# A chunked delta-rule recurrence on Trainium2: when the transposes, the norm's variance sums and the last inverse are issued, and where ScalarE copies the transposes

## The chip, the cores and the metric

The kernel runs on one core of one Trainium2 chip. The metric is the device time of one execution, in microseconds (us); the time before is the median of three runs.

## The reference

The program computes two blocks on a sequence of 512 tokens of width 1024, in float32. The first block has an RWKV-7 mixer (32 heads of size 64) and a short convolution; the second has a gated convolution, stick-breaking attention and a gated FFN. The change touches only the mixer's recurrence and the norm behind it:

```python
def wkv7_scan(r, decay, k, v, kk, kka):
    def step(S, inp):
        r_t, w_t, k_t, v_t, kk_t, kka_t = inp
        sa = jnp.einsum('bhvk,bhk->bhv', S, kk_t)
        S = (S * w_t[:, :, None, :] - sa[..., None] * kka_t[:, :, None, :]
             + v_t[..., None] * k_t[:, :, None, :])
        return S, jnp.einsum('bhvk,bhk->bhv', S, r_t)
...
def head_group_norm(y, w, b):
    mu = jnp.mean(y, axis=-1, keepdims=True)
    var = jnp.mean(jnp.square(y - mu), axis=-1, keepdims=True)
    yn = (y - mu) * lax.rsqrt(var + GN_EPS)
...
    y = wkv7_scan(rh, heads(decay), kh, vh, kk, kk * ah)
    y = head_group_norm(y, lnx_w, lnx_b)
    y = (y + bonus) * jax.nn.silu(g)
    return y @ w_out, v_first
```

## The kernel before

Most of the program is dense products of float32 numbers split into a high and a low part (lines 1948 to 1950). Between about 429 and 829 us runs the recurrence. It is chunked: 8 chunks of 64 tokens; within a chunk the step-by-step update becomes products of matrices and the inverse of a unit triangular matrix, and only a 64x64 state per head goes from chunk to chunk.

The 32 heads are cut into 8 turns of four heads (`PAIRS` = 8; two 128-row tiles `a` of two heads `h`). The loop has turns t = 0 to 8 and in each of them 24 steps s = 0 to 23. Three stages overlap as a pipeline:

- **Preparation of turn t.** It is done in four groups n (tile a, half g of the chunks, table `GROUPS`). For each group TensorE forms the products of queries and keys, `products` (line 576, 8 matmuls of 128 columns, 16 records), and transposes keys and values, `transposes` (lines 588 and 591, 8 matmuls). They work in PSUM banks 0 to 3 in alternation: products of group n use banks 2 and 3 where n is even and 0 and 1 where it is odd, transposes the other pair. So products of n wait until ScalarE has copied the transposes of n-1 (`turned_copied`), and transposes of n wait until VectorE has masked the products of n-1 (`products_masked`). VectorE masks with `first_steps` at step 2n and `second_steps` at step 2n+1 (lines 937 to 952). ScalarE copies the transposes in `turned_out` (bt, sv: 3 or 4 copies by the helper on line 832) and rounds in `rounded` (nixd, line 832). Steps 9 to 21 invert: `first_inverse`, five levels of `newton_v` (line 613, even steps) and `newton_x` (line 599, odd steps), whose results VectorE (`w`, line 1005, and one of four `inv`, line 787) and ScalarE (three of four `inv`) copy, then `residual` at step 20 and `last_inverse` at 21, whose results go into `tt`.
- **Chain of turn t-1.** `chain(t-1, s // 3, s % 3)`: each chunk takes three steps. Phase 0 (lines 523, 509, 529) forms the right side, phase 1 (line 542) multiplies it by the inverse `tt`, phase 2 (lines 550, 556) updates the state. After each phase `recurrence_evac` copies the result out of PSUM, half of the rows by VectorE (lines 758, 771) and half by ScalarE (line 759): `rhs`, then `sv` as u, then `sv` as the next state (two small copies on ScalarE). The next phase on TensorE waits for both halves.
- **Norm of turn t-2.** `norm_sum` (lines 690 and 693, one 128x512 float32 sum each in bank 4) centers and takes the variance of two tiles; ScalarE copies `sq`, squares into `acc` (line 904) and makes the inverse deviation (lines 908, 909); GpSimd ends the tile in `finish` (lines 1059 to 1062).

Each engine executes its own list in the order written, and a wait holds back all that stands behind it. TensorE's list in a step is: chain, then preparation, then norm sum. ScalarE's is: its part of the chain, `y_out` (the copy `tmp` of the y bank 7, line 832) at steps 0 and 12, its part of the preparation, its part of the norm:

```python
                    if when(t - 1, PAIRS):
                        recurrence_evac(act, 1, t - 1, s // 3, s % 3)
...
                    if when(t, PAIRS):
                        if s in (1, 3, 5, 7):
                            turned_out(t, s // 2)
                            rounded(t, s // 2)
```

SP issues the loads of later turns; each waits for the stage that frees its tile (`turned`, `y_summed`, `y_finished`).

Of the kernel before, what the change touches and what calls it, by code (L numbers as in the profile page):

```python
# [142 lines left out]
def program(nc, i, out):  # L143

    with ExitStack() as ctx:
# [340 lines left out]
        S_FIRST, S_LEVELS, S_RESIDUAL, S_LAST = 9, 10, 20, 21  # L486
        GROUPS = [(0, 0), (1, 0), (0, 1), (1, 1)]
        TURNED = [3, 6, 10, 14]

# [8 lines left out]
        def recurrence_tensor(pe, out_part):  # L498
# [62 lines left out]
            def products(t, n):  # L561

                (a, g), b = GROUPS[n], t % 2
                if n == 0:
                    pe.wait_ge(R["front_loaded"][b], LOAD_Q * (t // 2 + 1))
                    pe.wait_ge(R["keys_loaded"], LOAD_BC * (t + 1))
                    if t:
                        for h in range(2):
                            pe.wait_ge(R["inverse_made"][h], 2 * t)
                else:  # L570
                    if n == 2:
                        pe.wait_ge(R["back_loaded"][b], LOAD_Q * (t // 2 + 1))
                    pe.wait_ge(R["turned_copied"], TURNED[3] * t + TURNED[n - 1])
                for c in range(4):
                    for h in range(2):
                        last = mm(bank[product_bank(n, h)][:, c * P:(c + 1) * P], st_bc[rows[h], a, 4 * g + c, :, :],  # L576
                                  st_q[b][rows[h], a, h:h + 2, 4 * g + c, :], start=True, stop=True)
                last.then_inc(R["products_summed"], 1)

            def transposes(t, n):  # L580

                a, g = GROUPS[n]
                if n == 0:
                    pe.wait_ge(R["values_loaded"], LOAD_V * (t + 1))
                else:
# [71 lines left out]
            def last_inverse(t):  # L657

                for n, (a, g) in enumerate(GROUPS):
# [43 lines left out]
            for t in range(PAIRS + 1):  # L703
                for s in range(3 * NCH):
                    if t == 0 and s == 1:
                        pe.wait_ge(s_free[0], U_OUT1 // 2)
                        pe.wait_ge(s_free[1], U_OUT1 // 2)
# [81 lines left out]
        def recurrence_scalar(act, o, out_weights):  # L789
# [71 lines left out]

            for t in range(PAIRS + 2):
                b, q = t % 2, t - 2
                for s in range(3 * NCH):
                    if when(t - 1, PAIRS):
# [3 lines left out]
                    if s == 12 and when(t - 1, PAIRS):  # L869
                        y_out(t - 1, 0)  # L870
                    if when(t, PAIRS):
                        if s in (1, 3, 5, 7):
                            turned_out(t, s // 2)
# [19 lines left out]
                        elif s == S_LAST:  # L893
                            for n in range(2):
                                act.wait_ge(R["t_summed"], 4 * t + n + 1)
                                copy(tt[b][:, n, 0:4, :], heads(n)).then_inc(R["inverse_made"][0], 1)
                    if when(q, PAIRS):
                        if s in (2, 6):
                            a = s // 6
                            act.wait_ge(R["centered"], 2 * q + a + 1)  # L900
                            if q:
                                act.wait_ge(R["y_finished"], 2 * q - 1 + a)
                            o(copy(yc[a], bank[4][:]))
                            A(ysq[:], yc[a], ACT.Square).then_inc(R["y_squared"], 1)
                        if s in (4, 8):
                            a = s // 8
                            act.wait_ge(R["var_summed"], 2 * q + a + 1)
                            o(A(yr[a][:], bank[4][:], ACT.Ln, bias=eps[:, 1:2]))
                            A(yr[a][:], yr[a][:], ACT.Exp, scale=-0.5).then_inc(R["y_rstd_made"], 1)
                    then(t, s)  # L910

        def recurrence_vector(dve, o, out_weights):
# [66 lines left out]
            for t in range(PAIRS + 1):  # L979
                b = t % 2  # L980
                for s in range(3 * NCH):
# [34 lines left out]
                    elif s == S_LAST:  # L1016
                        for n in (2, 3):
                            dve.wait_ge(R["t_summed"], 4 * t + n + 1)
# [31 lines left out]
        def recurrence_gpsimd(gp, o):  # L1050
# [22 lines left out]
            for t in range(PAIRS + 2):  # L1073
# [5 lines left out]
                if when(t - 2, PAIRS):  # L1079
                    finish(t - 2, 0)  # L1080
# [3 lines left out]
                if when(t - 2, PAIRS):  # L1084
                    finish(t - 2, 1)
# [1662 lines left out]
```

## Time and profile before

| | |
|---|---|
| median of 3 runs | 2080.65 us (2079.68 to 2084.85) |
| profiled execution | 2086.95 us, its span 2085.2 us |
| TensorE busy (matmuls) | 2000.9 us, 96% |
| VectorE, ScalarE, GpSimd busy | 1395.0, 1032.0, 190.1 us |
| recurrence, turns 0 to 8 | about 429.6 to 829 us of the span |

The profile describes one execution. A busy share says how full an engine was, not what it held up; which engine sets the pace in a stretch is read from the waits in the timeline and from the chain of waits. In a timeline row the first number is the start, the second the time to the end of the last of the merged instructions; in brackets stands the idle time of the engine ahead of it and what ended it. A matmul shows twice: PEld is its weight load, PE the matmul itself. Matmul records of float32 count in passes (x16 for 8 matmuls of the program).

### The profile page before, as it was taken

What the parts mean: (1) busy time and instruction counts of PE and PEld (TensorE: products, weight loads), DVE (VectorE), ACT (ScalarE), POOL (GpSimd) and SP (SyncE); (2) the same over time, 40 slices, a digit from 0 to 9 for tenths busy, and PEclk for the clock granted to TensorE, in tenths of its full rate; (3) what the DMA queues carried; (4) which work ended last, traced back from release to release, by engine and by line L of the source; (5) the groups of instructions that cost most, each with busy time, mean ns of one, the idle gap of its engine ahead of it and who ended that gap; (6) DMA issues with size and microseconds to landing.
All of it is one profiled execution on the core that took longest, in us unless ns stands there. A gap on an engine that the chain in (4) does not pass through costs nothing.

```text
span 2085.2 us, 40330 instructions
## 1 busy us (share of the span) xinstructions
PE 2000.9 (96%) x15310; PEld 1609.8 (77%) x15310; DVE 1395.0 (67%) x2240; ACT 1032.0 (49%) x1829; POOL 190.1 (9%) x214
## 2 busy tenths in 40 slices
PE   5999999988889899999999999999999999999998
PEld 4877777777777776888888888888667778888886
DVE  7788888886566564555554556799777776455455
ACT  6666666666677675333322323442675434233243
POOL 4230000021343222100000000000000000000000
PEclk9999999999999999999999999999999999999999
DMA  4445555562334312233333333333113323333332
GB/s 120 119 142 162 178 185 174 176 155 75 95 84 99 81 56 82 87 96 94 97 101 92 100 91 100 101 91 100 40 43 107 95 61 91 97 95 95 97 93 78
DMA packets 371367, 215.02 MB, mean 103 GB/s; under 512 B 52369, under 2 KB 349737, under 8 KB 371241
## 3 DMA queue, kind: packets, MB, share of 16 engines
q1 hardware_dynamic: 371032, 213.18, 35.1%
q8 instruction: 91, 1.49, 0.3%
q14 instruction: 36, 0.29, 0.0%
q10 hardware_dynamic: 208, 0.06, 0.0%
HBM read 181.68 MB, written 31.52 MB: 102 GB/s over the span
## 4 chain that ended last, share of the span: by engine, by line
PE 88%; ACT 5%; DVE 4%; issue 2%; DMA 1%; SPq 1%; ACTq 0%; DVEq 0%
PE bank L1948 24%; PE bank L1950 23%; PE bank L1949 23%; PE bank L599 2%; PE bank L576 2%; PE bank L613 1%; PE bank L550 1%; PE bank L509 1%; ACT inv L832 1%; PE bank L523 1%; PE bank L588 1%; PE bank L1138 1%; PE bank L542 1%; PE bank L690 1%; PE bank L591 1%
## 5 line engine op out<-in xcount | busy, mean ns | idle before, releaser
L1948 PE MATMUL bank<-xl,w_hi 128*128 128x512 f32 x1568 | 615.6, 393 | 3.5 <-DVE xl L2670 2.5
L1949 PE MATMUL bank<-xl,w_lo 128*128 128x512 f32 x1568 | 611.2, 390 | 0.0
L1950 PE MATMUL bank<-xl,w_hi 128*128 128x512 f32 x1568 | 610.9, 390 | 0.0
L1595 ACT ACTIVATE w_hi<-w_raw 128x1024 fp32r<-128x1024 f32 x278 | 293.1, 1054 | 481.4 <-PE bank L1950 476.9
L2239 DVE TENSOR_TENSOR w_lo<-w_raw,w_hi 128x1024 fp32r<-128x1024 f32 x278 | 342.2, 1231 | 48.7 <-ACT w_hi L1595 40.1
L1948 PEld LDWEIGHTS bank<-xl,w_hi 128*128 128x128 f32 x1568 | 294.5, 188 | 76.6 <-issue 9.9
L1950 PEld LDWEIGHTS bank<-xl,w_hi 128*128 128x128 f32 x1568 | 294.8, 188 | 61.8
L1949 PEld LDWEIGHTS bank<-xl,w_lo 128*128 128x128 f32 x1568 | 294.7, 188 | 60.6 <-issue 0.5
L1948 PE MATMUL bank<-xh,w_hi 128*128 128x512 f32 x448 | 182.8, 408 | 12.2 <-DVE xh L2244 11.9
L1950 PE MATMUL bank<-xh,w_hi 128*128 128x512 f32 x448 | 175.2, 391 | 0.0
L1949 PE MATMUL bank<-xh,w_lo 128*128 128x512 f32 x448 | 175.0, 391 | 0.0
L1948 PEld LDWEIGHTS bank<-xh,w_hi 128*128 128x128 f32 x448 | 84.5, 189 | 33.9 <-issue 9.1
L1949 PEld LDWEIGHTS bank<-xh,w_lo 128*128 128x128 f32 x448 | 84.6, 189 | 18.1 <-issue 0.7
L1950 PEld LDWEIGHTS bank<-xh,w_hi 128*128 128x128 f32 x448 | 84.4, 188 | 17.9
L2514 DVE SCALAR_TENSOR_TENSOR dconv<-glu,par,dconv 128x512 f32<-128x512 f32 x120 | 83.1, 748 | 0.5
L832 ACT ACTIVATE inv<-bank 128x512 f16<-128x512 f32 (+1 forms) x152 | 73.3, 553 | 18.7 <-PE bank L599 16.8
L2244 DVE TENSOR_TENSOR xl<-tmp,xl 128x512 f32 (+1 forms) x62 | 42.1, 689 | 33.0 <-ACT xl L1923 17.9
L1005 DVE CAST_PREDICATED w<-bmask,bank 128x256 f16<-128x256 int32 x160 | 56.5, 417 | 6.7 <-PE bank L613 4.8
L787 DVE CAST inv<-bank 128x512 f16<-128x512 f32 x40 | 27.7, 692 | 44.9 <-PE bank L599 44.9
L1948 PE MATMUL bank<-y_part,w_hi 128*128 128x512 f32 x128 | 52.8, 413 | 0.0
L599 PE MATMUL bank<-inv,w 64*64 64x64 f16 x1280 | 46.7, 197 | 5.7 <-issue 5.7
L599 PE MATMUL bank<-w,inv 64*64 64x64 f16 x1280 | 47.3, 198 | 4.1 <-issue 3.9
(385 smaller groups left out, 3084.5 us busy)
## 6 DMA issues: line engine op xcount, KB each, us to landing
w_raw<-in_a_w_in SPq DMA_DIRECT2D x64, 512.0 KB, 4.2
w_raw<-in_b_w_in SPq DMA_DIRECT2D x64, 512.0 KB, 4.1
w_raw<-in_w_ffn_up SPq DMA_DIRECT2D x42, 512.0 KB, 3.9
w_raw<-in_w_in SPq DMA_DIRECT2D x36, 512.0 KB, 3.8
w_raw<-in_a_w_out SPq DMA_DIRECT2D x16, 512.0 KB, 3.8
w_raw<-in_b_w_out SPq DMA_DIRECT2D x16, 512.0 KB, 3.7
w_raw<-in_w_ffn_down SPq DMA_DIRECT2D x16, 512.0 KB, 3.7
d_g<-sq SPq DMA_DIRECT2D x16, 256.0 KB, 2.2
```

The costliest lines, as they stand in the source:

```text
L576: last = mm(bank[product_bank(n, h)][:, c * P:(c + 1) * P], st_bc[rows[h], a, 4 * g + c, :, :], st_q[b][rows[h], a, h:h + 2, 4 * g + c, :] ...
L599: last = mm(bank[n][hs, col0 + c * C:col0 + (c + 1) * C], lhsT[hs, 4 * g + c, :], rhs_[hs, 4 * g + c, :] if rhs_ is not eyes16 else eyes16 ...
L787: return copy(inv2[a][:, :, 4 * g:4 * g + 4, :], bank[n][:].rearrange("p (x c k) -> p x c k", x=2, c=4))
L832: return A(dst, src, ACT.Copy)
L1005: V.copy_predicated(w16[a][:, 4 * g:4 * g + 4, :], bmask[:, level, :].bitcast(I32).unsqueeze(1).to_broadcast([P, 4, C]), heads(n)).then_in ...
L1595: A(w_hi[0:rows, slot, 0:nkb, 0:ncol], w_raw[0:rows, slot, 0:nkb, 0:ncol], ACT.Copy).then_inc(s_hi, units)
L1948: mm(outp, wh, xlo, start=start, stop=False)
L1949: mm(outp, wl, xhi, start=False, stop=False)
L1950: return mm(outp, wh, xhi, start=False, stop=stop)
L2239: V.tensor_tensor(w_lo[part], w_raw[part], w_hi[part].bitcast(F32), ALU.subtract).then_inc(s_lo, units)
L2244: V.tensor_tensor(lo, tmp[:, buf, :], hi.bitcast(F32), ALU.subtract).then_inc(s_xlo, 1)
L2514: V.scalar_tensor_tensor(out=y, in0=glu[:, j, tap:tap + T], scalar=w, in1=y, op0=ALU.mult, op1=ALU.add).then_inc(s_tap, 1)
```

## The change

Nothing is computed otherwise; five things are issued in another order.

1. TensorE: `transposes` of group n follow `products` of the same group directly, at step 2n; they stood at step 2n+1.
2. ScalarE: `turned_out` of groups 1 to 3 stands at step 2n ahead of that step's `recurrence_evac`; `turned_out` of group 0 stands at step 0 behind it. `rounded` stays at step 2n+1. The `y_out` of step 12 moves to step 11.
3. Norm, in turns t < 8: the sums that center stay at steps 1 and (from 5 as before) 5, the sums of squares go from steps 3 and 7 to 11 and 15; on ScalarE center at 2 and 6, square at 4 and 14, inverse deviation at 12 and 16 (they were at 2, 6, 4 and 8, with the square right behind the centering). In turn 8 the steps stay as they were. GpSimd's `finish` of tile 0 moves behind its two `low_part`.
4. `last_inverse` is split: groups 2 and 3 at step 21, 0 and 1 at step 22; ScalarE's two copies `tt` go with the latter.
5. Waits follow: the products of a turn wait only for VectorE's half of the `tt` copies, the transposes for ScalarE's.

```diff
         S_FIRST, S_LEVELS, S_RESIDUAL, S_LAST = 9, 10, 20, 21
+        LAST_GROUPS = {S_LAST: (2, 3), S_LAST + 1: (0, 1)}
+        SUMS_LATE = {1: (0, False), 5: (1, False), 11: (0, True), 15: (1, True)}
+        SUMS_EARLY = {1: (0, False), 3: (0, True), 5: (1, False), 7: (1, True)}
+        NORM_LATE = {2: ("center", 0), 4: ("square", 0), 6: ("center", 1), 12: ("rstd", 0), 14: ("square", 1),
+                     16: ("rstd", 1)}
+        NORM_EARLY = {2: ("center_square", 0), 4: ("rstd", 0), 6: ("center_square", 1), 8: ("rstd", 1)}
...
 (products, n == 0)
-                        for h in range(2):
-                            pe.wait_ge(R["inverse_made"][h], 2 * t)
+                        pe.wait_ge(R["inverse_made"][1], 2 * t)
 (transposes, n == 0)
+                    if t:
+                        pe.wait_ge(R["inverse_made"][0], 2 * t)
...
 (norm_sum)
+                late = q + 2 < PAIRS
                 if not squares:
                     pe.wait_ge(R["y_bank_read"], 2 * q + 2)
-                    if q or a:
+                    if late and a:
+                        pe.wait_ge(R["y_squared"], 2 * q + 1)
+                    elif q or a:
                         pe.wait_ge(R["y_rstd_made"], 2 * q + a)
...
                 else:
+                    if late and a:
+                        pe.wait_ge(R["y_rstd_made"], 2 * q + 1)
+                    elif late:
+                        pe.wait_ge(R["r0_copied"], 4 * (q + 3))
                     pe.wait_ge(R["y_squared"], 2 * q + a + 1)
...
 (TensorE's step)
-                        if s < 8:
-                            (transposes if s % 2 else products)(t, s // 2)
-                            if t == 0 and s % 2:
-                                fill(4)
+                        if s < 8 and s % 2 == 0:
+                            products(t, s // 2)
+                            transposes(t, s // 2)
+                        elif s < 8 and t == 0:
+                            fill(4)
...
-                        elif s == S_LAST:
-                            last_inverse(t)
-                    if when(t - 2, PAIRS) and s in (1, 3, 5, 7):
-                        norm_sum(t - 2, s // 4, s % 4 == 3)
+                        elif s in LAST_GROUPS:
+                            last_inverse(t, LAST_GROUPS[s])
+                    if when(t - 2, PAIRS) and s in sums_of(t):
+                        norm_sum(t - 2, *sums_of(t)[s])
...
 (ScalarE's step)
+                    if when(t, PAIRS) and s in (2, 4, 6):
+                        turned_out(t, s // 2)
                     if when(t - 1, PAIRS):
                         recurrence_evac(act, 1, t - 1, s // 3, s % 3)
...
-                    if s == 12 and when(t - 1, PAIRS):
+                    if s == 11 and when(t - 1, PAIRS):
                         y_out(t - 1, 0)
                     if when(t, PAIRS):
-                        if s in (1, 3, 5, 7):
-                            turned_out(t, s // 2)
+                        if s == 0:
+                            turned_out(t, 0)
+                        elif s in (1, 3, 5, 7):
                             rounded(t, s // 2)
```

How the lists of the engines move is shown at two places of turn 2, which stands for turns 2 to 7. First ScalarE, steps 1 to 3, before: L759 is its part of the chain (waits `u_summed`, `s_summed`, `rhs_summed`), `bt` and `sv_132` the copies of the transposes (`turned`), `nixd` the rounding, `sq` and `acc` the norm.

```order
L759 ACTIVATE sv_133<-bank 64x2x64 [waits u_summed]
L832 ACTIVATE bt_144<-bank 128x512 [waits turned]
L832 ACTIVATE sv_132<-bank 64x4x64 x2
L832 ACTIVATE nixd_125<-nix_134 64x4x64 [waits nix_made]
L832 ACTIVATE nixd_125<-nix_134 64x4x64
L759 ACTIVATE sv_133<-bank,st_pc_140 64x64 [waits s_summed]
L759 ACTIVATE sv_133<-bank,st_pc_140 64x64
L832 ACTIVATE sq<-bank 128x512 [waits centered]
L904 ACTIVATE acc<-sq 128x512 [waits scalar_order]
L759 ACTIVATE rhs<-bank 64x128 [waits rhs_summed]
L832 ACTIVATE bt_144<-bank 128x512 [waits turned]
L832 ACTIVATE sv_132<-bank 64x4x64 x2
```

The same engine in the change (its helper lines are 781 for 759, 854 for 832), from step 0's copy of the transposes to step 3's right side:

```order
L854 ACTIVATE bt_144<-bank 128x512 [waits turned]
L854 ACTIVATE sv_132<-bank 64x4x64 x2
L781 ACTIVATE sv_133<-bank 64x2x64 [waits u_summed]
L854 ACTIVATE nixd_125<-nix_134 64x4x64 [waits nix_made]
L854 ACTIVATE nixd_125<-nix_134 64x4x64
L854 ACTIVATE bt_144<-bank 128x512 [waits turned]
L854 ACTIVATE sv_132<-bank 64x4x64 x2
L781 ACTIVATE sv_133<-bank,st_pc_140 64x64 [waits s_summed]
L781 ACTIVATE sv_133<-bank,st_pc_140 64x64
L854 ACTIVATE sq<-bank 128x512 [waits centered]
L781 ACTIVATE rhs<-bank 64x128 [waits rhs_summed,scalar_order]
```

The copies of group 1 (the second `bt`) stood behind the state copies and the rhs copy; they stand ahead of both.

Second TensorE, the same place in the change: steps 2 and 3 (L562 and L568 are phase 2 of the chain, L587 products, L604 and L607 transposes, L535 phase 0 of the next chunk).

```order
L562 MATMUL bank<-sv_132,bt_144 64x64 [waits u_copied1,u_copied0]
L562 MATMUL bank<-sv_132,bt_144 64x64 x3
L568 MATMUL bank<-ra_143,sv_132 64x64 x4
L587 MATMUL bank<-st_q_129,st_bc 128x128 [waits turned_copied]
L587 MATMUL bank<-st_q_129,st_bc 128x128 x7
L604 MATMUL bank<-ident,st_bc 128x128 [waits products_masked]
L604 MATMUL bank<-ident,st_bc 128x128 x3
L607 MATMUL bank<-ident,st_v 128x128 x4
L535 MATMUL bank<-sv_132,st_q_128 64x64 [waits s_copied1,s_copied0]
```

Before, L523 (now L535) with its wait for both state copies stood between L576 and L588, and a sum of squares (L693) behind L591.

## Rows read from the trace of the kernel before

**Rows 1.** The page: busy time, share and instructions of TensorE and ScalarE.
```profile
PE 2000.9 (96%) x15310; PEld 1609.8 (77%) x15310; DVE 1395.0 (67%) x2240; ACT 1032.0 (49%) x1829; POOL 190.1 (9%) x214
```
**Rows 2.** Stretches: length, busy of PE, PEld, DVE, ACT, POOL, clock; turns 1 and 3.
```profile
463.12:508.85 45.73, 38.03 (x985) 32.30 (x982) 30.20 (x84) 28.38 (x79) 6.95 (x8) 1.00 0.29 73
...
557.59:603.62 46.03, 41.37 (x994) 33.51 (x992) 28.55 (x81) 32.97 (x86) 15.31 (x15) 1.00 0.33 84
```
**Rows 3.** Stretches of turn 3: steps 0 to 8, 9 to 19; turn 1's steps 0 to 8.
```profile
557.59:576.92 19.33, 18.06 (x242) 13.30 (x239) 13.67 (x38) 15.45 (x42) 6.93 (x7) 1.00 0.15 39
576.92:597.80 20.88, 18.20 (x593) 15.58 (x593) 12.04 (x35) 14.91 (x38) 7.22 (x7) 1.00 0.58 149
...
463.12:482.97 19.85, 15.25 (x234) 12.39 (x229) 15.33 (x41) 12.13 (x37) 3.69 (x5) 1.00 0.05 10
```
**Rows 4.** Timeline of turn 3, steps 2 to 4, TensorE and ScalarE.
```profile
561.87 0.45 PE L550 MATMUL bank<-sv,bt 128*64 128x64 f32 x8
...
562.49 1.16 PE L576 MATMUL bank<-st_q,st_bc 64*128 64x128 f32 x16
...
563.61 0.54 PE L523 MATMUL bank<-sv,st_q 128*64 128x64 f32 x8
...
564.67 0.65 PE L588 MATMUL bank<-ident,st_bc 128*128 128x128 f32 x4
...
565.60 1.02 PE L693 MATMUL bank<-acc,head_mean 128*128 128x512 f32 x2
565.80 0.60 ACT L832 ACTIVATE bt<-bank 128x512 f32<-128x512 f32 x1 [0.55 <-PE bank L591]
...
566.55 0.45 PE L542 MATMUL bank<-rhs,tt 64*64 64x64 f32 x8
567.09 0.85 ACT L832 ACTIVATE nixd<-nix 64x256 f16<-64x256 f32 x2
```
**Rows 5.** Timeline of turn 3: GpSimd in step 5, the waits ahead of step 9.
```profile
569.57 1.28 POOL L1059 TENSOR_TENSOR y<-sq,yr_a 128x512 f32<-128x512 f32 x1 [11.97 <-ACT yr_a L909]
...
576.49 0.50 ACT L759 ACTIVATE sv<-bank,st_pc 64x64 f32<-64x64 f32 x2
...
576.92 0.54 PE L523 MATMUL bank<-sv,st_q 128*64 128x64 f32 x8 [1.07 <-ACT sv L759]
577.20 0.69 ACT L908 ACTIVATE yr_b<-bank,eps 128x512 f32<-128x512 f32 x1
```
**Rows 6.** Timeline of turn 3's inversion: steps 12 and 13, then 15 to 17.
```profile
584.17 0.45 PE L509 MATMUL bank<-st_q,sv 64*64 64x64 f32 x8 [0.51 <-ACT tmp L832]
...
589.87 0.42 PE L542 MATMUL bank<-rhs,tt 64*64 64x64 f32 x8
...
590.91 0.27 ACT L759 ACTIVATE sv<-bank 64x128 f32<-64x128 f32 x1
590.95 0.41 PE L613 MATMUL bank<-inv,nixd 128*128 128x64 f16 x8 [0.20 <-ACT inv L832]
591.82 0.51 ACT L759 ACTIVATE sv<-bank,st_pc 64x64 f32<-64x64 f32 x2 [0.63 <-PE bank L550]
```
**Rows 7.** Timeline of turn 3, steps 21 to 23, last inverse and what follows.
```profile
602.15 0.42 PE L542 MATMUL bank<-rhs,tt 64*64 64x64 f32 x8
...
603.11 0.45 PE L550 MATMUL bank<-sv,bt 128*64 128x64 f32 x8 [0.53 <-DVE sv L758]
```
**Rows 8.** Stretches by TensorE's clock: busy, then clock, DMA share, GB/s.
```profile
683.30:686.70 3.40, 1.60 (x76) 1.00 0.47 136
686.70:690.10 3.40, 3.17 (x45) 0.50 0.02 5
```
**Rows 9.** Timeline of TensorE: a product of the inversion at either clock.
```profile
583.02 0.64 PE L613 MATMUL bank<-inv,nixd 128*128 128x64 f16 x16
...
686.93 0.32 PE L599 MATMUL bank<-inv,w 64*64 64x64 f16 x4 [2.03 <-issue]
...
688.86 1.04 PE L613 MATMUL bank<-inv,nixd 128*128 128x64 f16 x16
```

More of the change, by code:

```diff
@@ L486, in program, with sums_of, norm_of @@
         S_FIRST, S_LEVELS, S_RESIDUAL, S_LAST = 9, 10, 20, 21
+        LAST_GROUPS = {S_LAST: (2, 3), S_LAST + 1: (0, 1)}
         GROUPS = [(0, 0), (1, 0), (0, 1), (1, 1)]
         TURNED = [3, 6, 10, 14]
+        SUMS_LATE = {1: (0, False), 5: (1, False), 11: (0, True), 15: (1, True)}
[3 more added lines that the diff above has]
+        NORM_EARLY = {2: ("center_square", 0), 4: ("rstd", 0), 6: ("center_square", 1), 8: ("rstd", 1)}
+        def sums_of(t):
+            return SUMS_LATE if t < PAIRS else SUMS_EARLY
+        def norm_of(t):
+            return NORM_LATE if t < PAIRS else NORM_EARLY
         def when(turn, last):
@@ L584, in transposes @@
                     pe.wait_ge(R["values_loaded"], LOAD_V * (t + 1))
+                    if t == 0:
+                        pe.wait_ge(s_free[0], U_OUT1 // 2)
+                        pe.wait_ge(s_free[1], U_OUT1 // 2)
+                    if t:
+                        pe.wait_ge(R["inverse_made"][0], 2 * t)
                 else:
@@ L655, in residual, with last_inverse @@
                     both_heads(n, nixd[a], inv2[a][:, 0], start=False).then_inc(R["e_summed"], 1)
-            def last_inverse(t):
-                for n, (a, g) in enumerate(GROUPS):
+            def last_inverse(t, groups):
+                for n in groups:
+                    a, g = GROUPS[n]
                     pe.wait_ge(R["e_copied"][n // 2], 2 * t + n % 2 + 1)
@@ L704, in recurrence_tensor @@
                 for s in range(3 * NCH):
-                    if t == 0 and s == 1:
-                        pe.wait_ge(s_free[0], U_OUT1 // 2)
-                        pe.wait_ge(s_free[1], U_OUT1 // 2)
                     if when(t - 1, PAIRS):
@@ L860, in y_out, with norm_part @@
                      bank[7][:].rearrange("p (a t) -> p a t", a=2)).then_inc(R["y_bank_read"], 1)
+            def norm_part(q, part, a):
+                if part.startswith("center"):
+                    act.wait_ge(R["centered"], 2 * q + a + 1)
+                    if q:
+                        act.wait_ge(R["y_finished"], 2 * q - 1 + a)
+                    o(copy(yc[a], bank[4][:]))
+                if part.endswith("square"):
+                    act.wait_ge(R["var_summed"], 2 * q + a)
+                    A(ysq[:], yc[a], ACT.Square).then_inc(R["y_squared"], 1)
+                if part == "rstd":
+                    act.wait_ge(R["var_summed"], 2 * q + a + 1)
+                    o(A(yr[a][:], bank[4][:], ACT.Ln, bias=eps[:, 1:2]))
+                    A(yr[a][:], yr[a][:], ACT.Exp, scale=-0.5).then_inc(R["y_rstd_made"], 1)
             for t in range(PAIRS + 2):
@@ L892, in recurrence_scalar @@
                                 copy(w16[n][:, 0:4, :], heads(n)).then_inc(R["e_copied"][0], 1)
-                        elif s == S_LAST:
+                        elif s == S_LAST + 1:
                             for n in range(2):
-                                act.wait_ge(R["t_summed"], 4 * t + n + 1)
+                                act.wait_ge(R["t_summed"], 4 * t + n + 3)
                                 copy(tt[b][:, n, 0:4, :], heads(n)).then_inc(R["inverse_made"][0], 1)
[L897 to L909, printed above, removed]
+                    if when(q, PAIRS) and s in norm_of(t):
+                        norm_part(q, *norm_of(t)[s])
                     then(t, s)
@@ L1017, in recurrence_vector @@
                         for n in (2, 3):
-                            dve.wait_ge(R["t_summed"], 4 * t + n + 1)
+                            dve.wait_ge(R["t_summed"], 4 * t + n - 1)
                             V.tensor_copy(tt[b][:, n - 2, 4:8, :], heads(n)).then_inc(R["inverse_made"][1], 1)
@@ L1078, in recurrence_gpsimd @@
                         G.tensor_copy(w16[a][:], eyes[:]).then_inc(R["units_reset"], 1)
-                if when(t - 2, PAIRS):
-                    finish(t - 2, 0)
                 if when(t, PAIRS):
@@ L1084, in recurrence_gpsimd @@
                 if when(t - 2, PAIRS):
+                    finish(t - 2, 0)
                     finish(t - 2, 1)
```

## The prediction

> **What bounds the kernel now.** I read the page first, for the size of things: TensorE is busy 96% of the span [rows 1]. That share is an average over dense products, which the change does not touch, and the recurrence. So next come the stretches of the recurrence, one turn each: turn 1, still without the norm, takes 45.73 us, a middle turn (turn 3) 46.03, with TensorE busy 41.37 and ScalarE 32.97 [rows 2]. Cut by steps [rows 3], its steps 0 to 8 take 19.33 us with TensorE busy 18.06 and ScalarE 15.45; steps 9 to 19, the inversion, take 20.88 with TensorE busy 18.20. So in steps 0 to 8 TensorE is nearly full, and every new wait there is added time; in the inversion a little room is left. The timeline then shows what the order does. Between phase 2 of the chain (561.87), the products (562.49), the next phase 0 (563.61), the transposes (564.67), the sum (565.60) and phase 1 (566.55) TensorE does not stop [rows 4]: while ScalarE and VectorE copy one thing, TensorE has another. The one long wait is at the end, 1.07 us ahead of 576.92, for ScalarE's state copies [rows 5].
>
> **The prices.** Issue time on TensorE, start to start [rows 4]: phase 2 of the chain 0.62, products 1.12, phase 0 1.06, transposes 0.93, a sum 0.95; phase 1 about 0.33 (its row's 0.45 less the latency; 0.28 more for line 509 every fourth chunk; phase 0 of a turn's first chunk only 0.70, as it lacks line 509). The transposes' result reaches ScalarE 1.13 after they start (564.67 to 565.80), so 0.20 after their last issue. `turned_out` then takes 1.29 (565.80 to 567.09), `rounded` 0.85 [rows 4]; the copy of a right side or of u 0.27 [rows 6], the pair of state copies 0.50 [rows 5]. From ScalarE's end to TensorE's start I take 0.1 to 0.2, the 0.20 of [rows 6].
>
> **Part 1, transposes and ScalarE's order, steps 0 to 8.** TensorE issues at an even step chain, products, transposes, and at the next odd step needs ScalarE's half of that chain part. ScalarE may copy it only behind `turned_out` of the same step, which waits for the transposes, although the chain's result has been there for two us. I lay the prices out from the start of the turn:
> - Step 0: phase 0 to 0.70, products to 1.8, transposes to 2.7. ScalarE copied the right side at 0.45 (here the chain is first), so phase 1 follows to 3.35 and the centering sum to 4.3. ScalarE: transposes' result 2.94, `turned_out` to 4.23, u copy to 4.5. TensorE starts phase 2 at 4.7: it waits 0.4.
> - Step 2: phase 2 to 5.3, products to 6.4, transposes to 7.36, result 7.56. `turned_out` to 8.85, the state copies to 9.4. TensorE waits from 7.36 to 9.45: 2.1 us.
> - Steps 3 and 4: phase 0 to 10.45, phase 1 to 10.85, products and transposes to 12.9, result 13.1; `turned_out` (four copies now, 1.33) to 14.4, u copy 14.7. TensorE goes on at 14.9: 2.0.
> - Steps 5 and 6: phase 2 and the second centering sum to 16.5, phase 0, products and transposes to 19.5, result 19.7, `turned_out` 21.05, right side 21.4. TensorE goes on at 21.5: 2.0.
> - Steps 7 and 8: phase 1 to 21.9, u copy by 22.3, phase 2 from 22.5 to 23.1; `rounded` of the last group keeps ScalarE until 23.2, the state copies follow, and step 9 begins at 23.7: two waits of 0.6.
>
> Check by sums: TensorE issues 15.9 us of work (the 18.06 busy less two sums of squares at 0.95, and within 0.3 of that), and waits 0.4 + 2.1 + 2.0 + 2.0 + 1.2 = 7.7; together 23.6 to 23.8 against 19.33. That is **+4.4 us** for each of turns 2 to 7. VectorE is never later than ScalarE in this: it is busy 13.67 of 19.33 [rows 3] with the same work, and its masks of a group end before the next transposes want them. Turn 1 has no norm: the same layout gives 23.15 where it took 19.85 [rows 3]: +3.3. Turn 0 has no chain, and its cycle (transposes, `turned_out`, next products) stays the same loop: 0. Turn 8 has no preparation: 0.
>
> **Part 2, the sums of squares in the inversion.** Two sums of 0.95 now stand at steps 11 and 15. At step 11 the sum delays the next phase 0 by 0.95, but TensorE no longer waits 0.51 for the y copy at 584.17 [rows 6], which ScalarE has made one step earlier: about +0.3. At step 15 the sum stands between line 599 and line 542 at 589.87; the last quarter of line 613 waited for ScalarE until 590.95 anyway [rows 6], which hides most, but phase 1's result comes later and VectorE's copies `w` queue behind its u copy: about +0.3. The inverse deviations (0.69 and 0.64 us; the first of the two in [rows 5]) leave step 8, where they held the right side at step 9 (-0.1), for 12 and 16; at 16 they push the state copies from 591.82 [rows 6] to about 593.2, still ahead of their use at about 594. Sum +0.5 a turn, bounds 0 (all hidden) and 1.9 (nothing hidden).
>
> **Part 3, the last inverse in two steps.** Its second half, 0.7 us, no longer stands ahead of phase 1 (602.15), nor VectorE's wait for it ahead of the u copy; phase 2 at 603.11 [rows 7], which waited 0.53 for VectorE, starts 0.6 earlier. ScalarE's `tt` copies run beside phase 2. -0.6 in each of turns 1 to 7. In turn 0 there is no chain to cover VectorE's residual copies, which groups 2 and 3 now want first: +0.6.
>
> **What moves and costs nothing.** GpSimd's `finish` starts behind steps 12 and 16 and takes four instructions of 1.28 [rows 5], some 5 us, done before the turn ends; the centering of the next turn wants it far later. SP's load of the norm's tiles waits for `finish` and so comes some 10 us later in the turn; behind it on that queue stands the load of the back half of the queries, which waits for the turn's last `y_summed` in any case. The y copy at 11 instead of 12: counted above, and in turn 1 worth -0.5.
>
> **The clock.** The stretch before 686.70 has TensorE busy 1.60 of 3.40 us, a stop of 2.03 us in it, and the next stretch has a granted clock of 0.50, the 1.2 GHz level [rows 8, 9]. So a stop as long as the three of part 1 has been followed by the lower level. What it costs: line 613 took 1.04 us instead of 0.64 [rows 9], a factor of 1.6; on the 2.05 us of products and transposes behind a stop that is up to 1.3 us, in the inversion next to nothing. Not every stop can meet it, since the waits for ScalarE also absorb some; I take one drop of 1.0 us a turn, 7 us in all. The bounds are 0 and 21 times 1.3, 27 us. The Trainium skill, page "TensorE: Matmul & The Clock Gate", section "A second HAM failure mode: psum-queue depth-cycling", says that short idle times between groups that cycle through PSUM banks can make the clock swing between its two levels again and again. By that rule the sum would take the upper bound.
>
> **Sum.** Turns 2 to 7: 4.4 - 0.1 + 0.5 - 0.6 = 4.2 each, 25.2. Turn 1: 3.3 - 0.5 - 0.6 = 2.2. Turn 0: 0.6. Together 28.0, with the clock 35. Against the profiled execution's 2086.95 us that is 2122; the median of the runs stands 6.3 us lower, at 2080.65, and I predict on it: **2115.7 us**.
>
> **The rivals.**
> - **A, the clock stays up**: or its drops fall where ScalarE is waited for anyway. For it: turn 3 has its 1.07 us wait at step 9 [rows 5] and stays at a full clock [rows 3]. 2080.65 + 28 = 2109. Chance 0.25.
> - **B, the clock swings in each group**: a drop behind each of the three stops, 7 x 3 x 1.3 = 27. For it: the one stop of 2 us in [rows 9]; against it: here two to three us of dense products and transposes stand between the stops. 28 + 27 = 55: 2136. This is the page's case. Chance 0.18.
> - **C, the sums do not hide**: the change does not do what it says, and in the inversion, busy 18.20 of 20.88 [rows 3], they cost 1.9 a turn in full, 1.4 more than taken, 8 in all on top of the forecast: 2124. Chance 0.07.
> - **D, faster**: TensorE's work is the bound in steps 0 to 8 and the copies come in time. Then each of turns 2 to 7 loses two sums, 1.9, and the wait of 1.07 there, pays 0.5, and gains 0.6 with every other at the end: 6 x -2.5 + 7 x -0.6 + 0.6, some -19, 2062. It decides where ScalarE has the chain part copied before TensorE has run out of work, that is if the step's `turned_out` plus copy (2.0 us from the last transpose) found 2.0 us of TensorE work behind the transposes. There is none at the even steps but 0. Chance 0.04, and 0.03 for no change in measure.
> - The forecast itself, one drop a turn: chance 0.43.
>
> **How the numbers follow.** About 0.3%, 6 us, is what a measurement of this kernel can tell from none. Slower are A, B, C and the forecast: 0.93; same 0.03; faster 0.04. The range reaches from 2100 (A, with part 1 smaller by 1.2 a turn) to 2138 (B).
>
> **What would show it.** Right: steps 0 to 8 of a middle turn take 23 to 26 us; three waits of TensorE for ScalarE's line 781 (`sv`, `sv`, `rhs`) near 2 us in each turn; phase 2 of step 23 a half us earlier; the inversion within 1 us of 20.88; a dip of the granted clock in most turns. Wrong: if the rows at steps 2, 4 and 6 show ScalarE's chain copy ahead of `turned_out`, or TensorE's waits there are under 1 us, part 1 falls; if the turn grows by over 7 us, the clock or the inversion was under-priced.

## The result and the profile after

The changed kernel took **2115.19 us** (median of 4 runs, 2111.81 to 2119.13), the kernel before 2080.58 (2079.68 to 2084.85, 4 runs beside them): a ratio of 1.0161, 95% interval 1.0143 to 1.018. It is slower, and the time forecast was 2115.7. The profiled execution took 2117.43 us with a span of 2115.7, against 2086.95 and 2085.2 before; the mean granted clock is 0.982 instead of 0.993. One of the later executions of the kernel before took 2500.86 us at a granted clock of 0.751; no comparison here uses it.

The page has the busy times of [rows 1]. TensorE's grew by 15.4 us with the same number of instructions, so about half of the 30.5 us of added span is slower work, and the rest is waiting.

```profile
PE 2016.3 (95%) x15310; PEld 1623.0 (77%) x15310; DVE 1394.8 (66%) x2240; ACT 1029.6 (49%) x1829; POOL 188.7 (9%) x214
```

The stretches of turn 1 and turn 3, then turn 3's steps 0 to 8, 9 to 19 and 20 to 23, turn 4's steps 0 to 8 and 9 to 19, and turn 1's steps 0 to 8 (columns as in [rows 2, 3]):

```profile
464.29:512.32 48.03, 37.71 (x986) 32.45 (x982) 29.67 (x83) 28.46 (x80) 6.18 (x7) 1.00 0.28 70
...
563.16:612.87 49.71, 43.36 (x994) 35.43 (x992) 28.60 (x81) 32.57 (x86) 14.94 (x15) 0.93 0.31 78
...
563.16:587.71 24.55, 18.57 (x239) 14.39 (x235) 13.54 (x38) 13.48 (x39) 3.38 (x5) 0.92 0.18 49
587.71:607.92 20.21, 19.86 (x596) 16.46 (x596) 12.21 (x36) 15.75 (x39) 10.15 (x10) 0.93 0.40 89
607.92:612.87 4.95, 4.93 (x165) 4.58 (x162) 2.84 (x8) 3.34 (x10) 1.41 (x2) 1.00 0.61 178
...
612.87:635.81 22.94, 17.05 (x238) 12.93 (x234) 13.55 (x38) 13.48 (x39) 3.37 (x5) 0.98 0.19 52
635.81:657.22 21.41, 21.06 (x597) 17.61 (x597) 12.29 (x36) 15.75 (x39) 10.17 (x10) 0.86 0.39 85
...
464.29:487.10 22.81, 15.04 (x235) 12.53 (x229) 14.55 (x40) 12.70 (x38) 3.85 (x5) 1.00 0.10 22
```

Steps 0 to 8 took 19.33 us in turn 3 [rows 3]; now they take 22.94 where the clock holds (turn 4) and 24.55 where it falls. For the whole recurrence, means over turns 2 to 7 (in brackets the least and the most of the six), of one profiled execution each:

| part of a turn | before | after | difference |
|---|---|---|---|
| steps 0 to 8 | 19.35 (19.33 to 19.39) | 24.26 (22.94 to 24.59) | +4.9 |
| steps 9 to 19 | 21.2 (18.66 to 23.94) | 20.9 (20.21 to 21.41) | -0.3 |
| steps 20 to 23 | 5.8 (5.45 to 6.19) | 5.4 (4.94 to 6.49) | -0.4 |

That makes 6 x 4.2 = 25. Turn 1 adds 2.3 (48.03 against 45.73), what lies ahead of turn 1 adds 1.2 and what lies behind turn 7 adds 1.7.

The timeline of turn 4, steps 2 to 4, is what [rows 4] was (line 832 is now 854, 759 is 781, 523 is 535, 550 is 562):

```profile
617.36 0.45 PE L562 MATMUL bank<-sv,bt 128*64 128x64 f32 x8
...
617.93 0.28 DVE L793 TENSOR_TENSOR sv<-bank,st_pc 64x128 f32<-64x128 f32 x1
617.98 1.16 PE L587 MATMUL bank<-st_q,st_bc 64*128 64x128 f32 x16
...
619.56 0.60 PE L607 MATMUL bank<-ident,st_v 128*128 128x128 f32 x4
...
620.20 0.60 ACT L854 ACTIVATE bt<-bank 128x512 f32<-128x512 f32 x1 [2.10 <-PE bank L607]
...
621.37 0.50 ACT L781 ACTIVATE sv<-bank,st_pc 64x64 f32<-64x64 f32 x2
...
621.81 0.54 PE L535 MATMUL bank<-sv,st_q 128*64 128x64 f32 x8 [1.65 <-ACT sv L781]
...
627.16 0.45 PE L562 MATMUL bank<-sv,bt 128*64 128x64 f32 x8 [1.67 <-ACT sv L781]
...
633.68 0.45 PE L554 MATMUL bank<-rhs,tt 64*64 64x64 f32 x8 [1.67 <-ACT rhs L781]
```

The chain's result is there at 617.93, when VectorE copies its half. ScalarE is idle for 2.10 us, then copies the transposes (620.20), and takes its half of the chain at 621.37, 3.4 us after VectorE. TensorE has run out of work at 620.16 and goes on at 621.81; its three stops in the turn are 1.65, 1.67 and 1.67 us long.

Last, the clock, which [rows 8] showed once: a stretch of turn 3 behind its first stop (step 2 to 3), and one across the start of turn 4's inversion; then the products of step 2 of turn 3, ahead of that stop, and those of step 4, in the slow stretch.

```profile
573.70:577.10 3.40, 3.40 (x23) 3.17 (x24) 1.88 (x7) 0.26 (x1) 0.00 (x0) 0.50 0.01 2
...
635.10:641.90 6.80, 6.40 (x140) 5.74 (x137) 2.97 (x11) 3.97 (x14) 2.30 (x2) 0.50 0.98 196
```
```profile
568.27 1.16 PE L587 MATMUL bank<-st_q,st_bc 64*128 64x128 f32 x16
...
573.61 2.07 PE L587 MATMUL bank<-st_q,st_bc 64*128 64x128 f32 x16
```

At 0.50, the 1.2 GHz level, the products take 2.07 us instead of 1.16. Over turns 2 to 7 the granted clock fell 11 times (3 times in turns 1 to 7 before): between 1.2 and 1.7 us after the end of the first stop in five of these turns, which slows step 4, and as long after the end of the third stop in all six, around step 9. It never fell behind the second.

### The profile page after: what moved, and what is told of

It is laid out like the page before. It is cut to its first block, busy times and chain, and to the rows that moved or that the text cites. A ratio compares the mean times of both kernels' runs of the same rounds, so it can differ in the third digit from the quotient of the medians.

```text
span 2115.7 us, 40352 instructions
## 1 busy us (share of the span) xinstructions
PE 2016.3 (95%) x15310; PEld 1623.0 (77%) x15310; DVE 1394.8 (66%) x2240; ACT 1029.6 (49%) x1829; POOL 188.7 (9%) x214
## 3 DMA queue, kind: packets, MB, share of 16 engines
q1 hardware_dynamic: 371032, 213.18, 34.6%
## 4 chain that ended last, share of the span: by engine, by line
PE 87%; ACT 6%; DVE 4%; issue 2%; DMA 1%; SPq 1%; POOL 0%; DVEq 0%; ACTq 0%; POOLq 0%
PE bank L1976 23%; PE bank L1978 23%; PE bank L1977 23%; PE bank L587 2%; PE bank L615 2%; PE bank L535 1%; PE bank L629 1%; ACT inv L854 1%; PE bank L521 1%; PE bank L604 1%; PE bank L562 1%; PE bank L554 1%; PE bank L1166 1%; ACT sv L854 1%; PE bank L717 1%
## 5 line engine op out<-in xcount | busy, mean ns | idle before, releaser
L854 ACT ACTIVATE bt<-bank 128x512 f32<-128x512 f32 x32 | 19.1, 597 | 74.5 <-PE bank L607 74.5
L1976 PE MATMUL bank<-y_part,w_hi 128*128 128x512 f32 x128 | 52.8, 412 | 0.0
L1977 PE MATMUL bank<-y_part,w_lo 128*128 128x512 f32 x128 | 50.0, 390 | 0.0
L1978 PE MATMUL bank<-y_part,w_hi 128*128 128x512 f32 x128 | 49.9, 390 | 0.0
```

Source lines behind the costliest of these rows:

```text
L854: return A(dst, src, ACT.Copy)
L1976: mm(outp, wh, xlo, start=start, stop=False)
L1977: mm(outp, wl, xhi, start=False, stop=False)
L1978: return mm(outp, wh, xhi, start=False, stop=stop)
```

## The experiments

Losses are ratios to the kernel before, run beside each; 0.001 is 2.1 us. The rows come from four sets of runs, the last three on different chips, and the kernel before has another median in each (2080.58 beside the change, 2084.5 beside the next four rows, 2086.10 beside the four after them, 2083.58 beside the last), so go by the ratios and not by the medians. "After" is the changed kernel. The segments are of one profiled execution each, turns 2 to 7. What was expected of each run was written before it, and after the result of the change was known.

| run | median us | ratio (95%) | steps 0 to 8 | steps 9 to 19 |
|---|---|---|---|---|
| after | 2115.19 | 1.0161 (1.0143 to 1.018) | 22.9 to 24.6 | 20.2 to 21.4 |
| chain copies first | 2102.46 | 1.009 (1.0063 to 1.0117) | 22.1 (one 23.8) | 20.2 to 21.5 |
| copies at odd steps | 2088.40 | 1.0014 (0.9999 to 1.0028) | 19.8 | 19.5 to 22.9 |
| TensorE kept busy | 2105.81 | 1.0109 (1.0089 to 1.0129) | 22.9 to 23.8 | 19.5 to 21.0 |
| norm as before | 2131.05 | 1.0219 (1.0194 to 1.0244) | 27.3 to 30.5 | 18.6 to 22.0 |
| split alone | 2083.30 | 0.9988 (0.9979 to 0.9996) | 19.34 | 18.8 to 23.4 |
| late norm alone | 2084.99 | 0.9996 (0.9987 to 1.0005) | 19.34 (one 20.6) | 19.5 to 20.8 |
| rounding at 8 | 2088.04 | 1.0013 (1.0002 to 1.0024) | 18.90 | 20.6 to 25.7 |
| split, y copy, rounding | 2087.35 | 1.0003 (0.9994 to 1.0011) | 18.90 | 20.3 to 24.3 |
| after without part 1 | 2081.08 | 0.9981 (0.9972 to 0.9991) | 19.4 (one 20.9) | 19.5 to 20.4 |

**The chain's copies ahead of the transposes'.** The change, with ScalarE's `turned_out` of steps 2, 4 and 6 behind the chain part of its step:

```diff
-                    if when(t, PAIRS) and s in (2, 4, 6):
-                        turned_out(t, s // 2)
                     if when(t - 1, PAIRS):
                         recurrence_evac(act, 1, t - 1, s // 3, s % 3)
+                    if when(t, PAIRS) and s in (2, 4, 6):
+                        turned_out(t, s // 2)
```

> The change, but ScalarE copies its chain part ahead of the transposes of the same even step. My theory: the change's time is lost where ScalarE's chain copies queue behind the copies of the transposes. At steps 2, 4 and 6 the three waits of TensorE near 1.7 us go, but since the transposes are still issued before the next odd step's chain part, that odd part now queues behind the copies: laid out by rows, steps 0 to 8 take 22 to 22.6 us against 22.9 to 24.6, so the total falls only by 5 to 15, to 2100 to 2110. Rival (it is the order within the even step alone): steps 0 to 8 fall to 19.3 or less and the total to 2085 or below.

As expected: steps 0 to 8 took 22.08 us, and 19.81 in turn 1. The three waits behind steps 2, 4 and 6 are gone, and others stand in their place. Turn 4, the stretch and the timeline at steps 2 and 3:

```profile
604.55:626.64 22.09, 16.72 (x239) 12.76 (x235) 13.80 (x38) 13.48 (x39) 3.28 (x5) 1.00 0.21 57
```
```profile
609.69 0.49 ACT L781 ACTIVATE sv<-bank,st_pc 64x64 f32<-64x64 f32 x2
...
611.88 0.60 ACT L854 ACTIVATE bt<-bank 128x512 f32<-128x512 f32 x1 [1.70 <-PE bank L607]
...
613.80 0.27 ACT L781 ACTIVATE rhs<-bank 64x128 f32<-64x128 f32 x1
...
614.22 0.45 PE L554 MATMUL bank<-rhs,tt 64*64 64x64 f32 x8 [1.39 <-ACT rhs L781]
```

Now the even step's copy is made at once (609.69), but the odd step's (613.80) stands behind the four copies of the transposes, and TensorE waits 1.39 us for it. The other long waits of the stretch are 1.54 us for the norm's `acc`, which also stands behind `turned_out` on ScalarE, and 2.05 us for the u copy. So the order at even steps costs 22.94 - 22.08 = 0.9 us a turn by itself; what else the turn gained is the clock, which stays up in steps 0 to 8 in all turns but the last.

**The copies at the odd steps.** The change, with `turned_out` of all groups at steps 1, 3, 5 and 7 behind the chain part, as before; the transposes stay behind the products:

```diff
-                    if when(t, PAIRS) and s in (2, 4, 6):
-                        turned_out(t, s // 2)
...
-                        if s == 0:
-                            turned_out(t, 0)
-                        elif s in (1, 3, 5, 7):
+                        if s in (1, 3, 5, 7):
+                            turned_out(t, s // 2)
                             rounded(t, s // 2)
```

> The change, but ScalarE's list has the copies of the transposes where they were before, at step 2n+1 behind its chain part; TensorE keeps the transposes behind the products. My theory: steps 0 to 8 take 19.5 to 20 us, as before, although two sums of 0.95 have left, since products of the next group now wait for the later copies; total 2074 to 2086. Rival (the transposes right behind the products cost by themselves): steps 0 to 8 stay above 22 and the total above 2100.

Steps 0 to 8 took 19.81. Of turn 4, the stretch and one copy at an odd step, with the product that needs it:

```profile
602.10:621.91 19.81, 16.79 (x238) 12.71 (x235) 13.61 (x38) 13.49 (x39) 3.28 (x5) 1.00 0.22 56
```
```profile
609.93 0.27 ACT L781 ACTIVATE rhs<-bank 64x128 f32<-64x128 f32 x1 [0.82 <-PE bank L535]
...
610.64 0.45 PE L554 MATMUL bank<-rhs,tt 64*64 64x64 f32 x8 [0.21 <-DVE rhs L780]
```

At these copies ScalarE now waits for the chain's result and not the other way round. The segments are as expected; the time of 2088.40 is 2.4 us above the upper end of what was, beside a kernel before that itself stood at 2084.5. From 1.0161 to 1.0014: nearly the whole loss is ScalarE's order, 2.3 us a turn of it in what stood behind the copies of the even steps (22.08 to 19.81).

**TensorE kept busy.** The change, with six products of constants behind the transposes of steps 2 and 4, into a bank that is free there; nobody reads their results. They fill the stops and leave the waits as they are.

```diff
                             transposes(t, s // 2)
+                            if t and s in (2, 4):
+                                keep_busy({2: 5, 4: 4}[s], 6)
```

> The change, plus six matmuls of 128x128 float32 (some 1.5 us, their result is not used) on TensorE behind the transposes at steps 2 and 4, into a bank that is free there, so that the engine works during two of the three waits. If the falls of the granted clock at step 4 come from those waits, they vanish, steps 0 to 8 take 22.9 in all turns, and the total falls by 5 x 1.6 = 8, to about 2107. If the clock costs nothing there: 2115, no change; if the added work delays the chain: above 2117.

The stretch of turn 2 and its timeline at step 2 (line 722 is the added work, 788 is 781):

```profile
511.77:534.71 22.94, 19.64 (x262) 15.68 (x258) 13.54 (x38) 13.47 (x39) 3.37 (x5) 1.00 0.17 44
```
```profile
518.89 1.50 PE L722 MATMUL bank<-mean_d,ident 128*128 128x128 f32 x12
...
520.70 0.55 PE L535 MATMUL bank<-sv,st_q 128*64 128x64 f32 x8 [0.30 <-ACT sv L788]
...
522.21 1.16 PE L587 MATMUL bank<-st_q,st_bc 64*128 64x128 f32 x16
```

The stop is 0.30 us instead of 1.65, the step is no later, the products behind it stay at 1.16 us, and the stretch is 22.94 where turn 2 of the change took 24.48. Four of the six turns are at 22.9 to 23.0, as was expected of all; the other two took 23.5 and 23.8. None of turns 2 to 7 has a drop of the clock in step 4 any more. The third stop was not filled (1.67 us, as before), and behind it the clock still falls, in five of the six turns: the drops follow the stops. More work on TensorE, 2.6 us a turn, made the kernel faster by 0.0052, some 11 us, where 8 were expected. In the profiled executions 6.4 us of it lie in steps 0 to 8 and 3.2 in the inversions of turns 2 to 7; turn 1, which had no drop in the change, gave another 1.8 that can't be the clock. What the filled stops gave back, apart from the waits, is thus the 6.4 us.

**The norm as before, inside the change** (sums at steps 3 and 7, square and deviations where they were):

```diff
         def sums_of(t):
-            return SUMS_LATE if t < PAIRS else SUMS_EARLY
+            return SUMS_EARLY
 
         def norm_of(t):
-            return NORM_LATE if t < PAIRS else NORM_EARLY
+            return NORM_EARLY
...
-                late = q + 2 < PAIRS
+                late = False
```

> The change, but with the norm's sums, squares and inverse deviations at the steps of before (1, 3, 5, 7 and 2, 4, 6, 8). My theory: the late sums are not what costs; back in steps 0 to 8 they lengthen these by some 2.5 us a turn (two sums, and ScalarE's 1.3 us pieces ahead of its chain copies) and give back about 0.5 in the inversion: total 2121 to 2131. Rival (sums in the inversion are the loss): below 2110.

Steps 0 to 8 of turn 4, and three rows of it:

```profile
622.20:649.52 27.32, 20.85 (x242) 14.25 (x239) 13.78 (x38) 15.44 (x43) 3.95 (x5) 0.92 0.18 44
```
```profile
632.57 2.07 PE L717 MATMUL bank<-acc,head_mean 128*128 128x512 f32 x2
...
640.42 1.10 PE L710 MATMUL bank<-tmp,center 128*128 128x512 f32 x2 [0.69 <-ACT yr_a L897]
...
647.48 1.13 PE L717 MATMUL bank<-acc,head_mean 128*128 128x512 f32 x2 [0.74 <-ACT acc L893]
```

In turn 4 the 4.4 us above the change's 22.94 can be read off (2.5 were expected): two sums of 0.95, two waits for ScalarE's norm work (0.69 and 0.74), and 1.05 because the first sum met the low clock (2.07 instead of 1.02, [rows 4]). So with part 1 in place the late norm saves: over turns 2 to 7 some 4.2 us a turn in steps 0 to 8, of which the inversion gives 1.2 back. A part of it is the clock, as steps 0 to 8 of turns 5 and 6 took 30.10 and 30.54 us at a granted clock of 0.83, and no turn of the change was under 0.92 there.

**The split alone** in the kernel before (`last_inverse` in two halves, at steps 21 and 22, with the copies and waits that follow):

```diff
-                        elif s == S_LAST:
-                            last_inverse(t)
+                        elif s in LAST_GROUPS:
+                            last_inverse(t, LAST_GROUPS[s])
```

> The kernel before, with the last inverse alone in two steps (groups 2 and 3 at step 21, 0 and 1 at step 22). My theory: steps 20 to 23 fall from 5.8 to 4.95 us in each of turns 1 to 7, steps 0 to 8 stay at 19.34; total 5 us less, 2076. Rival (what the split gives is lost again, as the next turn's products or the inverse's copies wait): 2081.

It gains 0.12%, 2.5 us, half of the 5 expected: steps 20 to 23 take 4.94 to 5.64 us, and 6.39 once, where they took 5.45 to 6.19.

**The late norm alone** in the kernel before (sums at 11 and 15, deviations at 12 and 16, y copy at 11, GpSimd's order; what the prediction calls part 2, of which the diff has the tables; the products' shorter wait of point 5 stayed too):

```diff
+        SUMS_LATE = {1: (0, False), 5: (1, False), 11: (0, True), 15: (1, True)}
+        NORM_LATE = {2: ("center", 0), 4: ("square", 0), 6: ("center", 1), 12: ("rstd", 0), 14: ("square", 1),
+                     16: ("rstd", 1)}
```

> The kernel before, with the late sums of squares, late deviations, GpSimd's order and the y copy at step 11, and nothing else of the change. My theory: taking two sums of 0.95 out of steps 0 to 8 gives next to nothing, since the loop of transposes, ScalarE's copies and next products then sets the pace: 19 to 20 us there, the inversion within 0.5; total 2079 to 2086. Rival (TensorE's work is the bound in steps 0 to 8): they fall to 17.5 and the total to 2070.

No change that can be measured, as expected, and steps 0 to 8 of turn 3 show why:

```profile
555.93:575.27 19.34, 16.45 (x238) 12.77 (x235) 13.55 (x38) 13.48 (x39) 2.51 (x4) 1.00 0.16 40
```
```profile
565.55 1.16 PE L587 MATMUL bank<-st_q,st_bc 64*128 64x128 f32 x16 [0.90 <-ACT sv L853]
...
573.51 0.45 PE L562 MATMUL bank<-sv,bt 128*64 128x64 f32 x8 [0.82 <-DVE sv L779]
...
575.27 0.54 PE L535 MATMUL bank<-sv,st_q 128*64 128x64 f32 x8 [1.07 <-ACT sv L780]
```

TensorE does 1.6 us less (16.45 against 18.06, [rows 3]) in the very same 19.34 us: two new waits (0.90, 0.82) have taken the sums' place, and the 1.07 of [rows 5] is still there. The 0.90 is the loop from the transposes over ScalarE's copies to the next products; the 0.82 and the 1.07 are the chain waiting for its own copies. These loops set the length, not TensorE's work.

**The rounding at step 8.** The kernel before, with `rounded` of the last group moved behind the state copies, to take away the wait of 1.07 us at step 9:

```diff
                             turned_out(t, s // 2)
-                            rounded(t, s // 2)
+                            if s < 7:
+                                rounded(t, s // 2)
                         elif s == 8:
+                            rounded(t, 3)
```

> The kernel before, with ScalarE's rounding of group 3 (0.85 us) moved from step 7 to step 8 behind the state copies. My theory: the wait of 1.07 us ahead of step 9 goes, steps 0 to 8 fall to 18.4, 7 turns x 0.9 = 6 us less, 2075. Rival (the wait turns up at the first products of the inversion, which need the rounding): 2081.

Steps 0 to 8 and 9 to 19 of turn 3:

```profile
559.51:578.41 18.90, 18.07 (x242) 13.28 (x239) 13.58 (x38) 15.01 (x40) 6.50 (x7) 1.00 0.14 37
578.41:600.42 22.01, 18.12 (x593) 15.50 (x593) 12.12 (x36) 15.46 (x39) 7.64 (x7) 1.00 0.59 143
```
```profile
581.05 0.45 PE L542 MATMUL bank<-rhs,tt 64*64 64x64 f32 x8 [1.09 <-ACT rhs L759]
```

The 0.44 us won at step 8, of 0.9 expected, comes back in step 10, as a wait of 1.09 us where it was 0.43: ScalarE's copy of the right side is later there. The ratio is 1.0013 (1.0002 to 1.0024), slower by no more than can just be told; 6 us less had been expected. This execution also has more of the stops of open cause that the last section describes, so the wait is not all of its longer inversion.

**Split, early y copy and rounding at 8** together in the kernel before (the edits of the two runs on them, and this):

```diff
-                    if s == 12 and when(t - 1, PAIRS):
+                    if s == 11 and when(t - 1, PAIRS):
                         y_out(t - 1, 0)
```

> The kernel before, with the last inverse in two steps, the y copy at step 11 and the rounding of group 3 at step 8 behind the state copies. My theory: three separate gains of 0.8, 0.4 and 0.9 us a turn, 7 x 2.1 = 15 less, 2066 to 2070. Rival (they share one slack): 2074 to 2078.

It came out at 1.0003, no gain, where 2066 to 2070 had been expected and even the rival said 2078 at most. The ratios of the two single runs, 0.9988 and 1.0013, multiply to 1.0001: what the split gains, the rounding seems to lose.

**The change without part 1**: transposes and ScalarE's copies at the odd steps as before; late norm, early y copy and split kept.

```diff
-                        if s < 8 and s % 2 == 0:
-                            products(t, s // 2)
-                            transposes(t, s // 2)
-                        elif s < 8 and t == 0:
-                            fill(4)
+                        if s < 8:
+                            (transposes if s % 2 else products)(t, s // 2)
+                            if t == 0 and s % 2:
+                                fill(4)
```

> The change without its first part: transposes at the odd steps and ScalarE's copies of them behind its chain part, as before; late sums, early y copy and the last inverse in two steps stay. My theory: the gains that the two kept parts show alone add up, since they lie in different steps: steps 0 to 8 at 19.34, 9 to 19 near 20, 20 to 23 near 5; some 0.2% to 0.4% below the kernel before. Rival (the time goes elsewhere, as with the rounding at step 8): no difference from before.

This has the lowest ratio of the study, 0.9981 (0.9972 to 0.9991), 4 us under the kernel before by the ratio and 2.5 by the medians; 0.2% to 0.4% had been expected. Its interval overlaps that of the split alone, so that the norm adds to the split's gain is not shown. Turn 3, steps 0 to 8 and 9 to 19:

```profile
553.97:573.33 19.36, 16.47 (x240) 12.79 (x235) 13.55 (x38) 13.52 (x40) 3.37 (x5) 1.00 0.20 59
573.33:592.84 19.51, 19.14 (x597) 15.62 (x597) 12.11 (x35) 15.84 (x40) 10.24 (x10) 1.00 0.47 105
```

Part 1 is thus more than the whole loss. By segments, at a full clock: transposes behind the products 0.45 (19.36 to 19.81), what stands behind ScalarE's even-step copies (the odd steps' chain part, and the norm's `acc`) 2.3, the even steps' chain part behind them 0.9, together 3.6 us a turn; the clock adds 1.6 in five turns of six, and more in the inversion.

## Why the prediction was right, point by point

- **Part 1, +4.4 a turn: the mechanism is shown, the size was 0.8 too large.** At a full clock it is 22.94 - 19.34 = +3.6. The layout set TensorE going again at 9.45, 14.9, 21.5 and 23.7 us; in turn 4 these are 8.94, 14.29, 20.81 and 22.94. The layout was half a microsecond too late by step 2 already: phase 2 came at 4.49 instead of 4.7 with no wait ahead of it (0.4 was laid out), `turned_out` took 1.17 and not 1.29, the rest is in the hand-overs. The later steps add 0.1 each to the error. The idle times are 1.65, 1.67 and 1.67 where the layout said 2.1, 2.0 and 2.0 with the latency of a start in them. Moving the copies alone (22.94, 22.08, 19.81) shows that ScalarE's order makes them. In turn 1, +3.3 forecast and +2.96 measured, one sentence of the layout fails: VectorE is later than ScalarE there, and TensorE waits 1.53 us for it at 469.42 (it waited 0.51 before).
- **"TensorE is nearly full" was wrong as a reason.** The late norm alone took two sums out of steps 0 to 8 and left them at 19.34. A busy share of 93% did not make TensorE's work the bound: the loop through ScalarE was as long. The sum escaped this, as it laid out the new loop and did not add waits to the old length, but the premise of rival D falls: without part 1 the sums save nothing there.
- **Part 2, +0.5 and -0.1 a turn: too small, but inside its bounds.** Inversions without a stop or a drop took 18.66 (before, turn 6) and 18.78 (split alone), with the sums 19.51 (four of the six in the change without part 1): +0.8, in the bounds of 0 and 1.9. In the means it is not seen, since TensorE's irregular stops (last section) added less in this execution than in that of before.
- **Part 3, -0.6 a turn: right, a bit small.** Phase 2 of step 23 no longer waits for VectorE, and the stretch takes 4.95 us in four of six turns, -0.8 against the mean of before. Turn 5's 6.49 has a stop of 1.45 in it. Turn 0's +0.6 can't be told from the scatter, as turn 1 begins between 463.1 and 466.1 us in the runs.
- **The clock, 7 us: right in kind, under-priced.** One drop of 1.0 a turn was laid out. There were two, and that in step 4 costs 1.6 (24.55 against 22.94; five of them, 8 us): the layout took the factor 1.6 of a small f16 product [rows 9], where the float32 products are 1.8 times as long (2.07 against 1.16). Filling the first two stops gave back 6.4 of it in steps 0 to 8. Around step 9 the inversion takes 20.2 or 21.4 with a drop, against 19.51 without: 0.7 or 1.9, about 8 in all. Together some 16 of the 27 that the upper bound allowed. The Trainium skill, page "TensorE: Matmul & The Clock Gate", section "A second HAM failure mode: psum-queue depth-cycling", says that the clock can swing again and again where such idle times recur; the trace agrees in that (11 drops in six turns), but not at each stop: behind the second of the three it never fell. No run here tells whether the banks have a part in it.
- **The sum.** For turns 2 to 7 the terms with the clock gave 5.2 each; the two profiled executions differ by 4.2. They differ by 30.5 us in all, the medians by 34.6, because that of before had stood 6.3 above its median and that of after stands 2.2 above. And the three to four runs that gave 2080.6 for the kernel before lie low: the later sets of 12, 35 and 15 runs have medians of 2083.58 to 2086.10, next to that profiled execution. So the forecast of 35 is near the medians to half a microsecond by luck; the terms are right to about 1 us a turn, and their errors (part 1 too large, clock too small, inversion's stops fewer) cancel.
- **The rivals.** A (the clock stays up, or falls where it costs nothing, 2109) falls by the rows at 0.50 and by the 1.6 us of a drop in step 4. B (a drop behind each stop, 2136) falls by their number, two of three, and by their price, 16 us and not 27. C falls, since the sums cost 0.8 and not 1.9. D falls by its own point of decision: in turn 4 TensorE runs out of work 1.65 us before ScalarE has the chain part copied.

## What to carry to other kernels

When two engines hand work back and forth in a fixed order, put the copy that the other engine needs next first, and the bulk copies behind it: what is ready must not queue behind something that has still to be waited for. A busy share of 93% on one engine does not say that less work there helps; take a piece of it out and see whether the stretch gets shorter. And test a change of several parts part by part: here two parts were together worth about 4 us, and the third cost some 37.

## What was not expected of the hardware

The clock fell in streams that stood for 1.65 us only: 11 times in turns 2 to 7. The same stop can pass without: turn 4 has the same three, and no drop in step 4. In the run with the norm as before even turn 1 had drops behind two of its stops (steps 0 to 8 in 25.78 us, granted clock 0.85), and none in the change (22.81, 1.00), though turn 1 has no norm and its instructions are the same in both. What decides between the two is open.

The other is left open too: mostly inside the streams of small products in the inversion TensorE stands for up to 2.4 us at a time, with nothing in the trace that it waits for, as [rows 9] show once. These stops sum to 12.6 us over the recurrence before, 5.8 after, 5.5 with TensorE kept busy and 16.2 with the rounding at step 8, and a good part of the scatter of the inversion (18.66 to 23.94 us before) is theirs. Over the eleven kernels they fall into two groups: 12.6 to 17.4 us in the kernel before, the split alone, the rounding at step 8 and the three edits together, 5.5 to 9.5 in the other seven. The seven have GpSimd's `finish` behind `low_part` (point 3 of the change), and the four don't; the place of the norm does not divide them, since the run with the norm as before has 6.2. No run moves GpSimd's order alone, and each sum is of one execution, so a cause is not shown. But the shorter inversion of the change without part 1 may in part be this.
